# A hybrid convolution and state-space block on one core: what stands ahead of block 0, and where the rest of the modulation is made

## The chip, the cores and the metric

The kernel runs on one core of a Trainium2 chip. The metric is device time in microseconds (us), the median of several runs. Five engines work side by side, each through its own list in order: TensorE (PE, matmuls; its weight loads are PEld), VectorE (DVE), ScalarE (ACT), GpSimd (POOL) and SyncE (SP, which here only issues DMAs). Semaphores join the lists.

## The reference

One sequence of 2048 rows and width 1024 in float32, one layer. A vector `c` gives six modulation vectors of 1024 through `w_ada` (1024 x 6144, 24 MB):

```python
mod = (silu(c) @ w_ada + b_ada)
sh1, sc1, g1, sh2, sc2, g2 = split(mod, 6)
h = rmsnorm(x, norm1_g) * (1 + sc1) + sh1
u_conv, u_ssm, gl_conv, gl_ssm = split(h @ w_in)          # 1024, 512, 1024, 1024 columns
y_conv = silu(layernorm(causal_conv31(a * sigmoid(gate)))) @ conv_proj   # a, gate = split(u_conv)
y_ssm  = za * sigmoid(zb)      # za, zb = split(gelu(S5(u_ssm)) @ ssm_glu)
x = x + g1 * ((sigmoid(gl_conv) * y_conv + sigmoid(gl_ssm) * y_ssm) @ w_out)
h = rmsnorm(x, norm2_g) * (1 + sc2) + sh2
x = x + g2 * ((silu(f_gate) * f_up) @ w_ffn_out)          # f_gate, f_up = split(h @ w_ffn_in)
return rmsnorm(x, final_g)
```

S5 is a diagonal complex state space: 32 groups of 16 channels with 64 states each, computed in chunks of 8 steps. Its tables are made on the chip: an input matrix (`wm`), an output matrix (`vm`), the short kernel inside a chunk (`kst`), and the sine and cosine tables `sin_t`, `cos_t`.

## The kernel before

The sequence is worked in four blocks of 512 rows through the mixers (function `mixers`), then all rows go through the feed-forward part, which neither code nor diff touches here. Every float32 product of a layer is three matmuls (high by high, low by high, high by low: `three`, L1513 to L1515), so weights are split into `w_hi` and `w_lo`. A weight chunk is 512 KB. SP loads it into one of three `raw` buffers, POOL splits it with two instructions (L1793, L1795) into one of two slots, and PE uses it for 24 matmuls. POOL may split chunk w only when PE is done with chunk w-2. There are 48 chunks a block; here they are numbered 0 to 47.

On PE a block runs: four layers `us` (the S5 input), two pairs `ua`/`ug` (the gated convolution's input), `S` (state inputs, 4 quarters), two more pairs, gates `gl0` to `gl4`, a wait for the rotated states, `Y0` to `Y3` with a gate after each, gates to `gl15`, then `za`, `zb`, `cp`, and the output product with the transposes `h0` to `h7` of the next block's rows between. DVE runs: `u0`, 13 taps of the convolution, `u1`, 7 taps, then for each quarter q of the state the rotation `Rt`, `Rc`, `Rs` and the scan `sc` (L767 to L776), back-rotations `Dt`, `Dc`, `Ds` (L787 to L792), 104 more taps (L740), the low parts `ysl` of the S5 output (L558), and elementwise work. `u{m}` is one multiplication (L725) that waits for ACT's sigmoid of layer `ug{m}`. In the loop `u2` stands behind the scan of quarter 0 and `u3` behind that of quarter 2. PE's `Y0` waits for `Ds3`, its `za0` for `ysl3`.

Ahead of block 0 is the prologue. SP loads `w_ada` in 24 slabs of 1 MB into three buffers that lie over the `raw` and split buffers (`SLABS`, L1853); so weights of block 0 can be loaded only when the slabs are done. PE takes 20 slabs (`modulation`, L1445 and L1449), POOL four (L1769, L1763). Between them PE makes `h` of block 0 from transposed rows, transposes `wm`, and computes the `kst` tiles (L1505). DVE computes the tables in one long chain; each of its links waits for the one before. ACT stores `wm`, `vm` and `kst` to DRAM (L1107, L1109, L1113), from where SP loads them as needed. Every block's ACT list begins with a wait for these stores:

```python
act.wait_ge(wt_out, 16)
act.wait_ge(mat_out, 16 * (1 + T))
```

Blocks 0 to 2 are a hardware loop on PE, DVE and ACT (`Fori`), block 3 is written out; SP loops over all four.

Of the kernel before, what the change touches and what calls it, by code (L numbers as in the profile page):

```python
# [18 lines left out]
class Steps:  # L19

    def __init__(self, sem, phases):
        self.sem, self.at, self.base, self.per, self.names = sem, {}, {}, {}, {}
        total = 0
        for phase, times, segments in phases:
            n = 0
            names = []  # L30
            for seg, rep in segments:
                for j, name in enumerate(seg):
                    assert (phase, name) not in self.at, name
                    self.at[phase, name] = (n + j + 1, len(seg))
                names += seg
                n += len(seg) * rep
            self.base[phase], self.per[phase], self.names[phase] = total, n, names
            total += n * times
        self.next = {phase: 0 for phase, _, _ in phases}

    def step(self, phase, name):

        want = self.names[phase][self.next[phase]]
        assert want == name, f"{phase}: {name} where {want} stands"
        self.next[phase] += 1
        return self.sem, 1

    def again(self, phase):

        self.finished()  # L50
        self.next[phase] = 0

    def after(self, phase, b, name, it=0):

        at, width = self.at[phase, name]
        return self.sem, self.base[phase] + at + b * self.per[phase] + it * width

    def before(self, phase, b, name, it=0):

        at, width = self.at[phase, name]  # L60
        round_ = self.per[phase] if it is None else width
        v = self.base[phase] + at - round_
        assert v >= 0, (phase, name, v)
        return self.sem, v + b * self.per[phase] + (0 if it is None else it * width)

    def start(self, phase, b):

        return self.sem, self.base[phase] + b * self.per[phase]

    def finished(self):  # L70
        for phase, n in self.next.items():
            assert n in (0, len(self.names[phase])), (phase, self.names[phase][n])


def build(nc, x, c, w_ada, b_ada, norm1_g, w_in, conv_w, conv_b, conv_ln_g, conv_ln_b, conv_proj,
# [22 lines left out]
    ADA = 3  # L98


    SLABS = [("pe", k, h, r) for k in range(5) for h in range(2) for r in range(2)]
    for n, at in enumerate((2, 7, 12, 17)):
        SLABS.insert(at, ("pool", 5, n // 2, n % 2))
    last_slab = lambda kind: SLABS.index(("pe", kind, 1, 1))
    first_gate = last_slab(1) + 1
# [49 lines left out]
    with ExitStack() as ctx:  # L155
# [11 lines left out]
        def align():  # L167
# [20 lines left out]
            ("zero1", "eps1", "half_pi", "sign", "nsign")))  # L188
        ss, sd, rs, ss2, sd2, rs2 = (place(n, [P, TT], at=unit_at + 160 + 32 * i) for i, n in enumerate(
# [3 lines left out]
        bmod, c_in, ng = vt[:, 0:6 * KD], vt[:, 6 * KD:7 * KD], vt[:, 7 * KD:9 * KD]  # L193
# [88 lines left out]
        modrow = place("modrow", [4, HALF], at=ptmp_at)
        jexp = place("jexp", [P, T + 1, G])
        jer = place("jer", [P, T + 1, G])
        jei = place("jei", [P, T + 1, G])
        sv = place("sv", [P, 12, G])
        iota_i = place("iota_i", [P, NC + 1], I32)
        iota_f = place("iota_f", [P, NC + 1])
        cact = place("cact", [P, KD])
        dvec = place("dvec", [HG, G])  # L290
        cbc = place("cbc", [P, KD, P])
        ones = place("ones", [P, P])
        zc = place("zc", [P, KD, 7])
        ddiag = place("ddiag", [HG, G, HG])
        nat_v = place("nat_v", [6 * KD + 3 * KD + 3 * KC, P])
        nat_a = place("nat_a", [2 * G, P])
        nat_w = place("nat_w", [KC * TAPS, P])

        kst_at = end_kept - (T - 1) * G * HG * 4
        assert cursor[0] <= kst_at, (cursor[0], kst_at)  # L300
        kst = place("kst", [HG, G, 2 * T - 1, HG], at=kst_at)
        ada = [place(f"ada{s}", [P, KD // 2, HALF], at=raw_at + s * KD * HALF * 2) for s in range(ADA)]

        acc = place("acc", [P, 2, HALF], at=raw_at + ADA * KD * HALF * 2)
        bg = place("bg", [P, 2, D], at=dt_at)
        cursor[0] = h_at
        karg = place("karg", [P, 2, NC + 1, G])
        ktmp = place("ktmp", [P, NC + 1, G])
        jarg = place("jarg", [P, 2, T + 1, G])
        jtmp = place("jtmp", [P, T + 1, G])  # L310
        assert cursor[0] <= tr_at
# [17 lines left out]
        GY, GE = 5, 11  # L329
# [3 lines left out]
        pe_mix = [f"us{m}" for m in R(KS)] + [f"u{a}{m}" for m in R(2) for a in "ag"]  # L333
        pe_mix += [f"S{q}" for q in R(NQ)] + [f"u{a}{m}" for m in R(2, KC) for a in "ag"] + gl(0, GY)
        for q in R(NQ):
            pe_mix += [f"Y{q}", f"gl{GY + q}"]
        pe_mix += gl(GY + NQ, 2 * KD)
        for p in R(KD // 2):
            pe_mix += [f"za{m}" for m in pair(p)] + [["ln1"], ["ln2"], [], []][p] + [f"zb{m}" for m in pair(p)]
        pe_mix += [f"cp{m}" for m in R(KD)]  # L340
        for f in R(2):
            for j in R(KD // 2):
                pe_mix += [f"oc{f}{j}"] if j < KD // 2 - 1 else [f"o{f}{i}" for i in R(TT)]
                pe_mix += [f"h{k}" for k in TURN[j]] if f == 0 else []
# [10 lines left out]
        for q in R(NQ):  # L355
            act_mix += [f"Y{q}", f"gl{GY + q}"]
# [13 lines left out]
        for q in R(NQ):  # L370
            dve_mix += [f"Rt{q}", f"Rc{q}", f"Rs{q}", f"sc{q}"] + [["u2"], [], ["u3"], []][q]
# [1638 lines left out]
```

## Time and profile before

| | us |
|---|---|
| median of 3 runs | 2778.56 (2777.52 to 2779.61) |
| profiled execution, own time | 2779.5 |
| its span, first to last instruction | 2777.4 |
| PE busy | 2628.7 (95%) |
| DVE, ACT, POOL busy | 1508.4, 724.5, 1706.9 |
| mean granted PE clock | 0.973 of full speed |

Busy time is the union of an engine's instructions; issuing DMAs and waiting do not count. A timeline row gives start, duration, the line in the kernel's source, operation, output and inputs, and in brackets how long the engine was idle before it and what ended that. PE's instructions show two records for a plain float32 matmul.

### The profile page before, as it was taken

The page shows a single profiled execution, that of the slowest core. Times are in us where ns is not written, and L with a number is a line of the kernel's source. Part 1 is how long each engine was busy: PE and PEld are TensorE (multiplying, and loading weights), DVE is VectorE, ACT ScalarE, POOL GpSimd, SP SyncE. Part 2 cuts the span into 40 slices and gives each one's busy share as a digit, 9 for nine tenths or more (in the row PEclk, how much of TensorE's full clock was granted, in tenths as well). Part 3 has the DMA queues.
Part 4 walks back from the last instruction along what each step waited for, and adds up shares of the span by engine and source line. Part 5 has one row for each costly group of instructions (what it writes and reads, how often), then busy time and mean ns, then how long its engine had stood idle before and what let it go on. Part 6 is the DMA issues. An engine that isn't in the chain of part 4 may idle for free.

```text
span 2777.4 us, 32161 instructions
## 1 busy us (share of the span) xinstructions
PE 2628.7 (95%) x11735; PEld 2134.4 (77%) x11735; DVE 1508.4 (54%) x1772; ACT 724.5 (26%) x1116; POOL 1706.9 (61%) x1085
## 2 busy tenths in 40 slices
PE   4769999999999999999989999999999999999998
PEld 0347778878887878877868888878888878888886
DVE  6806975399629963597753334373333334735531
ACT  2210152103411232114533335443333321201100
POOL 2335465555666465546577776778777756766664
PEclk9888999999999999999999999999999999999999
DMA  8477443755276534835232232323222237556542
GB/s 259 167 197 149 113 148 121 176 152 159 92 194 148 158 106 138 195 111 187 82 115 87 73 107 85 120 69 91 73 88 87 73 110 258 185 178 192 169 128 76
DMA packets 422357, 376.20 MB, mean 135 GB/s; under 512 B 91752, under 2 KB 329528, under 8 KB 422072
## 3 DMA queue, kind: packets, MB, share of 16 engines
q1 hardware_dynamic: 312640, 294.69, 35.2%
q10 hardware_dynamic: 109560, 79.41, 10.8%
q8 instruction: 100, 1.64, 0.3%
q14 instruction: 57, 0.47, 0.1%
HBM read 311.06 MB, written 54.53 MB: 132 GB/s over the span
## 4 chain that ended last, share of the span: by engine, by line
PE 80%; DVE 10%; DMA 2%; ACTq 2%; issue 2%; POOL 2%; ACT 1%; DVEq 0%; SPq 0%; POOLq 0%
PE bank L1513 17%; PE bank L1515 17%; PE bank L1514 17%; PE bank L1718 5%; PE bank L1720 5%; PE bank L1719 5%; DVE wst L789 2%; PE bank L1634 2%; PE bank L1636 2%; PE bank L1635 2%; DVE bank L767 1%; PE bank L1575 1%; PE bank L1576 1%; PE bank L1562 1%; ACTq L1113 1%
## 5 line engine op out<-in xcount | busy, mean ns | idle before, releaser
L1793 POOL CAST w_hi<-raw 128x1024 fp32r<-128x1024 f32 x192 | 216.1, 1125 | 559.9 <-PE bank L1515 459.1
L1795 POOL TENSOR_TENSOR w_lo<-raw,w_hi 128x1024 fp32r<-128x1024 f32 x192 | 486.0, 2531 | 15.4
L1513 PE MATMUL bank<-h_hi,w_hi 128*128 128x512 f32 x896 | 356.9, 398 | 20.4 <-ACT uz L1142 19.4
L1514 PE MATMUL bank<-h_lo,w_hi 128*128 128x512 f32 x896 | 353.3, 394 | 0.0
L1515 PE MATMUL bank<-h_hi,w_lo 128*128 128x512 f32 x896 | 353.2, 394 | 0.0
L740 DVE SCALAR_TENSOR_TENSOR bank<-uc,cwt,bank 128x512 f32<-128x512 f32 x464 | 328.4, 752 | 8.0
L1812 POOL TENSOR_TENSOR fw_lo<-fsum,fw_hi 128x512 fp32r<-128x512 f32 x176 | 234.0, 1331 | 106.1 <-ACT fw_hi L1305 106.1
L1513 PE MATMUL bank<-xc_hi_T,fw_hi 128*128 128x512 f32 x704 | 276.2, 392 | 7.4 <-DVE tr L911 6.0
L1718 PE MATMUL bank<-ow_hi,hid_hi 128*128 128x512 f32 x704 | 274.6, 390 | 3.8 <-DVE hid_lo L971 3.8
L1515 PE MATMUL bank<-xc_hi_T,fw_lo 128*128 128x512 f32 x704 | 275.0, 391 | 0.0
L1514 PE MATMUL bank<-xc_lo_T,fw_hi 128*128 128x512 f32 x704 | 275.0, 391 | 0.0
L1719 PE MATMUL bank<-ow_hi,hid_lo 128*128 128x512 f32 x704 | 274.6, 390 | 0.0
L1720 PE MATMUL bank<-ow_lo,hid_hi 128*128 128x512 f32 x704 | 274.6, 390 | 0.0
L1513 PEld LDWEIGHTS bank<-h_hi,w_hi 128*128 128x128 f32 x896 | 171.8, 192 | 58.2 <-ACT uz L1142 19.8
L1513 PE MATMUL bank<-xc_hi_B,fw_hi 128*128 128x512 f32 x528 | 208.0, 394 | 7.2 <-issue 3.8
L1515 PE MATMUL bank<-xc_hi_B,fw_lo 128*128 128x512 f32 x528 | 207.0, 392 | 0.0
L1514 PE MATMUL bank<-xc_lo_B,fw_hi 128*128 128x512 f32 x528 | 206.9, 392 | 0.0
L1515 PEld LDWEIGHTS bank<-h_hi,w_lo 128*128 128x128 f32 x896 | 171.0, 191 | 36.7
L1514 PEld LDWEIGHTS bank<-h_lo,w_hi 128*128 128x128 f32 x896 | 171.4, 191 | 35.1
L971 DVE TENSOR_TENSOR hid_lo<-hraw,hid_hi 128x512 fp32r<-128x512 f32 x88 | 142.5, 1657 | 88.3 <-ACT hid_hi L1393 88.3
L1812 POOL TENSOR_TENSOR fw_lo<-raw,fw_hi 128x512 fp32r<-128x512 f32 x110 | 150.2, 1366 | 59.9 <-ACT fw_hi L1305 59.9
L1840 POOL TENSOR_TENSOR ow_lo<-raw,ow_hi 128x1024 fp32r<-128x1024 f32 x66 | 169.2, 2563 | 5.3
(291 smaller groups left out, 4975.6 us busy)
## 6 DMA issues: line engine op xcount, KB each, us to landing
raw<-in_w_in SPq DMA_DIRECT2D x112, 512.0 KB, 4.7
raw<-in_w_ffn_in SPq DMA_DIRECT2D x66, 512.0 KB, 5.5
raw<-in_w_ffn_out SPq DMA_DIRECT2D x66, 512.0 KB, 4.4
ada<-in_w_ada SPq DMA_DIRECT2D x24, 1024.0 KB, 5.2
hid_scratch<-tr SPq DMA_DIRECT2D x88, 256.0 KB, 2.6
hraw<-hid_scratch SPq DMA_DIRECT2D x88, 256.0 KB, 3.9
ssm_m<-vk_scratch SPq DMA_DIRECT2D x32, 512.0 KB, 4.9
raw<-in_ssm_glu SPq DMA_DIRECT2D x32, 512.0 KB, 3.6
```

Source lines behind the costliest of these rows:

```text
L740: ins = v.scalar_tensor_tensor(out=dst, in0=src, scalar=w, in1=conv_bank(m)[:], op0=ALU.mult, op1=ALU.add)
L971: v.tensor_tensor(hid_lo[n % RING][:], hraw[n % 4][:], hid_hi[n % RING][:].bitcast(F32), ALU.subtract).then_inc(hid_lo_done, 1)
L1513: t.matmul(dst, wh, xh, start=first, stop=False)
L1514: t.matmul(dst, wh, xl, start=False, stop=False)
L1515: return t.matmul(dst, wl, xh, start=False, stop=last)
L1718: t.matmul(dst, hid_hi[hs][:, cols], ow_hi[slot][:, wcols], start=(k == 0), stop=False)
L1719: t.matmul(dst, hid_lo[hs][:, cols], ow_hi[slot][:, wcols], start=False, stop=False)
L1720: ins = t.matmul(dst, hid_hi[hs][:, cols], ow_lo[slot][:, wcols], start=False, stop=(k == KF - 1))
L1793: g.tensor_copy(hi[:], src[:]).then_inc(hi_done, 1)
L1795: g.tensor_tensor(lo[:], src[:], hi[:].bitcast(F32), ALU.subtract).then_inc(split_done, 1)
L1812: g.tensor_tensor(fw_lo[i][:], part[WEIGHTS[i]], fw_hi[i][:].bitcast(F32), ALU.subtract)\
L1840: g.tensor_tensor(lo[:], src[:], hi[:].bitcast(F32), ALU.subtract).then_inc(ow_lo_done, 1)
```

## The change

The prologue keeps what block 0's first layer needs. Only `sh1` and `sc1` (8 slabs, 8 MB) are made there, by PE, with four buffers that lie in memory used later, so `raw` is free from the start. The small loads are reordered: `c` and the vectors, then `x`, then the S5 poles (`nat_a`), `log_dt` and the b inputs; four more kinds of small loads go to SP behind the first three weight chunks. `norm_roots`, `norm_scale` and ACT's statistics go ahead of the S5 tables. The transposition of `wm`, the c inputs, `sin_t`/`cos_t`, `vm`, `kst` and the DRAM stores go into block 0, among its input layers. On DVE the table work keeps its operands `first`, `second` and `part` in PSUM banks. In the DRAM copy of `kst` zeros are stored once, and each of the 8 stores of `kst` (ACT) writes only its non-zero part.

The other four modulation vectors are made one a block (`MADE`): eight slices of `w_ada` of 512 KB and the bias, broadcast, pass the `raw` ring, one behind each third weight chunk up to number 26. POOL multiplies each with its part of `silu(c)` and adds it into `acc` (`part_of_ada`), and PE sums over partitions behind `cp1` (`ad0`, `ad1`); ACT copies the result.

All loops over blocks are written out. In block 0 all four input pairs stand ahead of `S`, and seven gates instead of five stand ahead of `Y0`. In blocks 1 to 3 `u2` and `u3` move behind the scans of quarters 1 and 3.

```diff
-    ADA = 3
+    ADA = 4
+    SLABS = [(k, h, r) for k in range(2) for h in range(2) for r in range(2)]
...
+        MIX_CHUNKS.append(key)
+        if w % 3 == 2 and w // 3 <= KD:
+            MIX_CHUNKS.append(("ada", w // 3))
...
-        GY, GE = 5, 11
+        GY, GE = [7, 5, 5, 5], [12, 11, 11, 11]
...
+        MADE = ["g1", "sh2", "sc2", "g2"]
...
+            gated(0, 0)
+            dve.wait_ge(*scal.after("pro", "m8"))
+            link(v.tensor_copy(mag_k[:, :, 1:], mag_t[:].unsqueeze(2).broadcast_to([P, G, NC])))
+            dve.wait_ge(*tensor.after(0, "ct1"))
+            link(v.tensor_scalar(bank[4][:], bank[4][:], nsign[:, 0:1], None, ALU.mult))
+            link(v.tensor_scalar(bank[5][:], bank[5][:], -1.0, None, ALU.mult))
+            for j in R(4):
+                output_matrix(j)
+            gated(0, 1)
+            for j in R(4, T + 1):
+                output_matrix(j)
+            gated(0, 2)
...
-                    if q in (0, 2):
-                        gated(2 + q // 2)
+                    if b and q % 2:
+                        gated(b, 2 + q // 2)
...
+            def store_kernel():
+                act.wait_ge(pro_v, mark["kst"])
+                act.wait_ge(zeros_in, 16)
+                for t in R(T):
+                    act.dma_start(vk_d[t * HG:(t + 1) * HG, :, 1, t * HG:],
+                                  kst[:, :, 0:T - t, :].rearrange("p g s h -> p g (s h)")).then_inc(mat_out, 16)
...
-                act.wait_ge(wt_out, 16)
-                act.wait_ge(mat_out, 16 * (1 + T))
...
+                        if b == 0 and name == "us0":
+                            pe.wait_ge(*vec.after("pro", f"hl{k}"))
...
+                if b == 0:
+                    state_matrix()
+                    conv_input(*R(KC))
+                    kernel_tiles()
+                else:
+                    conv_input(0, 1)
...
+            def part_of_ada(b, n, k):
+                src = raw[n % RAW][:]
+                factor = cact[:, k:k + 1] if k < KD else part128[:, 0:1]
+                if k:
+                    g.tensor_scalar(src, src, factor, None, ALU.mult).then_inc(ada_scaled, 1)
+                    pool.wait_ge(ada_scaled, KD * b + k)
+                    pool.wait_ge(split_done, RAW + b * NMIX + ada_place[k - 1] + 1)
+                    g.tensor_tensor(acc[:], acc[:], src, ALU.add).then_inc(split_done, 1)
+                else:
+                    if b:
+                        pool.wait_ge(*tensor.after(b - 1, ad(b - 1)[-1]))
+                    g.tensor_scalar(acc[:], src, factor, None, ALU.mult).then_inc(split_done, 1)
```

PE from `sh1`/`sc1` to the first layer of block 0. Before, the slabs of the other vectors, the transposed `wm` and the `kst` tiles (`vm,b`) stand between `h` (the 32 transposes of `xs`) and the first layer:

```order
L1469 MATMUL bank<-ident,modrow 128x4 x4
L1476 MATMUL bank<-ident,cx 128x128 x8
L1459 MATMUL bank<-ident,xs 128x128 x32
L1445 MATMUL bank<-ada_245,cbc 128x512 x4
...
L1489 MATMUL bank<-ident,wm 128x128 x32
...
L1498 MATMUL bank<-acc,ones 128x512 x2
L1505 MATMUL bank<-vm,b_221 16x128 x32
...
L1513 MATMUL bank<-h_hi,w_hi_52 128x512
```

The change, same place; the rows of `wm` and `vm` stand behind 4 and 12 layers (`h_hi`, `w_hi`) of block 0:

```order
L1439 MATMUL bank<-ident,modrow 128x4 x4
L1452 MATMUL bank<-ident,xs 128x128 x32
L1423 MATMUL bank<-ident,nat_w 128x124
L1488 MATMUL bank<-h_hi,w_hi_52 128x512
...
L1467 MATMUL bank<-ident,wm 128x128 x32
L1473 MATMUL bank<-ident,cx 128x128 x8
L1488 MATMUL bank<-h_hi,w_hi_52 128x512
...
L1482 MATMUL bank<-vm,b_235 16x128 x32
L1543 MATMUL bank<-u_116,ssm_m_95 128x64 x8
```

So nothing but one transpose of the taps now stands between `h` and the first layer, and the `kst` tiles run directly ahead of `S`.

DVE in block 1, from the rotation of quarter 0; `dt_62` to `dt_65` are the quarters, `uc<-bank,tr_60` is `u2`. Before (a looped block):

```order
L767 TENSOR_TENSOR bank<-dt_62,sin_t 128x512
L769 TENSOR_TENSOR wst<-wst,cos_t 128x8x64
...
L725 TENSOR_TENSOR uc<-bank,tr_60 128x512
L767 TENSOR_TENSOR bank<-dt_63,sin_t 128x512
```

The change:

```order
L745 TENSOR_TENSOR bank<-dt_62,sin_t 128x512
L747 TENSOR_TENSOR wst<-wst,cos_t 128x8x64
L750 TENSOR_TENSOR wst<-wst,bank 128x8x64
L754 SCALAR_TENSOR_TENSOR wst<-mag_k,zero_70,wst 128x520
L745 TENSOR_TENSOR bank<-dt_63,sin_t 128x512
...
L644 TENSOR_TENSOR uc<-bank,tr_60 128x512
L745 TENSOR_TENSOR bank<-dt_64,sin_t 128x512
```

`u2` moved from ahead of quarter 1 to ahead of quarter 2.

POOL in block 0 of the change, where before there are only pairs of CAST and TENSOR_TENSOR of weight chunks:

```order
L1782 CAST w_hi_53<-raw_49 128x1024
L1784 TENSOR_TENSOR w_lo_55<-raw_49,w_hi_53 128x1024
L1761 TENSOR_SCALAR raw_50<-raw_50,vt 128x1024
L1764 TENSOR_TENSOR acc<-acc,raw_50 128x1024
L1782 CAST w_hi_52<-raw_51 128x1024
```

Behind each third split two instructions for `w_ada` stand in the list.

## Rows read from the trace of the kernel before

**Rows 1.** The page: busy time, share of the span and instructions of each engine.

```profile
PE 2628.7 (95%) x11735; PEld 2134.4 (77%) x11735; DVE 1508.4 (54%) x1772; ACT 724.5 (26%) x1116; POOL 1706.9 (61%) x1085
```

**Rows 2.** Windows: us; busy PE, PEld, DVE, ACT, POOL; clock; DMA share; GB/s. Blocks 0 and 1.

```profile
156.00:494.00 338.00, 306.51 (x1379) 255.44 (x1380) 202.26 (x251) 73.03 (x103) 174.17 (x96) 0.92 0.55 147
494.00:796.00 302.00, 294.14 (x1381) 245.31 (x1381) 208.47 (x256) 73.24 (x102) 173.13 (x96) 0.98 0.52 147
```

**Rows 3.** Timeline of PE in the prologue and block 0: start, us, operation, count, idle before.

```profile
15.39 0.34 PE L1433 MATMUL bank<-ident,nat_a 64*128 64x64 f32 x1 [15.39 <-DMA nat_w<-in_conv_w]
...
36.72 13.90 PE L1449 MATMUL bank<-ada,zc 128*4 128x512 f32 x32 [1.90 <-DMA ada<-in_w_ada]
...
100.71 7.19 PE L1445 MATMUL bank<-ada,cbc 128*128 128x512 f32 x16 [1.79 <-DMA ada<-in_w_ada]
...
123.58 3.71 PE L1489 MATMUL bank<-ident,wm 128*128 128x128 f32 x32
...
147.70 7.75 PE L1505 MATMUL bank<-vm,b 128*16 128x128 f32 x64
...
156.40 0.49 PE L1513 MATMUL bank<-h_hi,w_hi 128*128 128x512 f32 x1 [0.96 <-ACT kst L1102]
...
197.87 0.80 PE L1513 MATMUL bank<-h_hi,w_hi 128*128 128x512 f32 x1 [19.40 <-ACT uz L1142]
```

**Rows 4.** Timeline of ACT and its DMA issues (ACTq), end of the prologue.

```profile
157.19 30.92 ACTq L1113 DMA_DIRECT2D vk_scratch<-kst  x8
195.49 1.28 ACT L1142 ACT_TABLE_LOAD   x1 [39.42 <-DMA vk_scratch<-kst]
```

**Rows 5.** Timeline of PE: last layers of block 0, its end, and block 1.

```profile
378.14 0.49 PE L1513 MATMUL bank<-ys_hi,w_hi 128*128 128x512 f32 x1 [0.57 <-POOL w_lo L1795]
...
494.36 0.49 PE L1513 MATMUL bank<-h_hi,w_hi 128*128 128x512 f32 x1
...
538.00 1.22 PE L1562 MATMUL bank<-u,ssm_m 128*128 128x64 f32 x10
...
600.70 0.68 PE L1575 MATMUL bank<-wst,ssm_m 128*128 128x64 f32 x2 [6.09 <-DVE carry L797]
...
680.17 0.49 PE L1513 MATMUL bank<-ys_hi,w_hi 128*128 128x512 f32 x1 [0.64 <-ACT sg_s L1168]
```

**Rows 6.** Timeline of DVE in block 1: rotations, scans and what follows.

```profile
546.86 1.11 DVE L767 TENSOR_TENSOR bank<-dt,sin_t 128x512 f32<-128x512 f32 x1
...
556.90 0.69 DVE L725 TENSOR_TENSOR uc<-bank,tr 128x512 f32<-128x512 f32 x1 [5.85 <-ACT tr L1153]
557.51 3.36 DVE L767 TENSOR_TENSOR bank<-dt,sin_t 128x512 f32<-128x512 f32 x1
...
599.79 0.69 DVE L792 TENSOR_TENSOR wst<-wst,bank 128x512 f32<-128x512 f32 x1
...
675.26 4.69 DVE L558 TENSOR_TENSOR ys_lo<-tr,ys_hi 128x512 fp32r<-128x512 f32 x4
```

**Rows 7.** Windows, columns as before: the slab loads; GB/s is last.

```profile
25.00:50.00 25.00, 21.94 (x47) 4.13 (x48) 23.97 (x31) 3.38 (x6) 6.75 (x5) 1.00 0.90 317
```

**Rows 8.** Timeline of DVE in the prologue: the low parts of h.

```profile
82.26 0.69 DVE L558 TENSOR_TENSOR h_lo<-bank,h_hi 128x512 fp32r<-128x512 f32 x1
...
85.04 0.69 DVE L558 TENSOR_TENSOR h_lo<-bank,h_hi 128x512 fp32r<-128x512 f32 x1
```

**Rows 9.** Timeline of POOL in the same stretch: both halves of a weight chunk's split.

```profile
550.93 1.04 POOL L1793 CAST w_hi<-raw 128x1024 fp32r<-128x1024 f32 x1 [9.16 <-PE bank L1515]
552.05 2.39 POOL L1795 TENSOR_TENSOR w_lo<-raw,w_hi 128x1024 fp32r<-128x1024 f32 x1
556.37 1.04 POOL L1793 CAST w_hi<-raw 128x1024 fp32r<-128x1024 f32 x1 [1.93 <-PE bank L1515]
...
562.93 3.22 POOL L1795 TENSOR_TENSOR w_lo<-raw,w_hi 128x1024 fp32r<-128x1024 f32 x1
```

**Rows 10.** Windows, columns as before: PE behind its wait for the rotations; clock ahead of DMA share.

```profile
600.00:610.00 10.00, 9.30 (x38) 8.84 (x39) 9.61 (x16) 0.60 (x1) 0.00 (x0) 0.51 0.12 25
```

More of the change, by code:

```diff
@@ L66, in start, with step @@
-    def start(self, phase, b):
-        return self.sem, self.base[phase] + b * self.per[phase]
+        for stage, names in stages:
+            self.next[stage] = 0
+            for name in names:
+                total += 1
+                assert (stage, name) not in self.at, name
+                self.at[stage, name] = total
+    def step(self, stage, name):
+        want = self.names[stage][self.next[stage]]
+        assert want == name, f"{stage}: {name} where {want} stands"
+        self.next[stage] += 1
+        return self.sem, 1
@@ L294, in build @@
[L294 to L311, printed above, removed]
+        def early(at, end, *buffers):
+            cursor[0] = at
+            made = [place(*b) for b in buffers]
+            assert cursor[0] <= end, (buffers[0][0], cursor[0], end)
+            return made
@@ L894, in mixers @@
                     residual(1)
+                if MADE[b] == "sc2":
+                    dve.wait_ge(*scal.after(b, "ad0"))
+                    scale_of(1)
                 return residual
[L897 removed]
+            for b in R(NB - 1):
                 mixers(b)
[L899 removed]
             last_residual = mixers(NB - 1, last=True)
@@ L1453, in transposes @@
-            def transposes(phase, b, k, free=True):
+                t.transpose(dst[:, 0:rows], src[:], ident[0:rows, 0:rows]).then_inc(*tensor.step("pro", f"v{n}"))
+            pe.wait_ge(vectors_in, 7 * 16)
+            turn_rows_in(1, nat_v, bank[1])
+            pe.wait_ge(poles_in, 64)
+            turn_rows_in(0, nat_a, bank[0])
+            pe.wait_ge(pro_v, mark["zc"])
+            for n, (kind, half, rows) in enumerate(SLABS):
+                pe.wait_ge(ada_in[n % ADA], 16 * (n // ADA + 1))
+                for j in R(KD // 2):
+                    k, r = rows * KD // 2 + j, 2 * kind + half
+                    ins = t.matmul(bank[7][0:4, :], zc[:, k, 3 - r:7 - r], ada[n % ADA][:, j, :],
+                                   start=(r == 0 and k == 0), stop=(r == 3 and k == KD - 1))
+                ins.then_inc(*tensor.step("pro", f"ada{n}"))
@@ L1454, in transposes, with wait_bank @@
+            pe.wait_ge(pro_v, mark["modrow"])
+            for j in R(4):
+                ins = t.transpose(bank[7][:, 4 * j:4 * j + 4], modrow[:, j * P:(j + 1) * P], ident[0:4, 0:4])
+            ins.then_inc(*tensor.step("pro", "mt"))
+            def wait_bank(stage, name):
+                free = bank_free(stage, name)
                 if free:
-                    pe.wait_ge(*bank_free(phase, b, f"h{k}"))
+                    pe.wait_ge(*free)
+            def transposes(stage, k):
+                wait_bank(stage, f"h{k}")
```

1174 lines of the change are left out of this document (563 added, 611 removed).

## The prediction

> **What bounds the kernel now.** I read four views. The page first: PE is busy for 95% of the span [rows 1], so only two things can move the time much: where PE stands idle, and where it works at half clock. The windows by stage then show where that is: block 0 takes 338 us and PE is busy in 306.5 of them, block 1 takes 302 with 294.1 [rows 2]; and block 0 begins only at 156.40 [rows 3]. Blocks 2 and 3 take within 1 us of block 1. The timeline of PE tells what it does ahead of block 0: 16 matmuls (two records each), which are four slabs, in 13.90, the transposes of `wm` 3.71, the `kst` tiles 7.75, and long waits between; the wait of 19.40 at 178 is inside block 0 [rows 3]. The last is due to ACT: it issues the stores of `kst` for 30.92 us, stands idle 39.42 until they have landed, and reaches block 0's first own work at 195.49 [rows 4]. Last, the rows around one block [rows 5, 6]: PE waits 6.09 for the rotated states at 600.70, and DVE, busy otherwise through the rotations, waits 5.85 for ACT's `tr`, that is for `ug2`, which it had reached too early. `ysl3` ends at 675.26 + 4.69 = 679.95 and `za0` starts at 680.17: from the rotations on, DVE's chain and PE end almost together. So from the state inputs to `za0` DVE sets the pace, elsewhere PE.
>
> **Part 1, the slabs that stay.** Eight slabs in one stretch, all early. One slab costs 13.90/4 = 3.47 [rows 3]. Their loads fit: 317 GB/s came in while slabs were loaded [rows 7], 3.3 us for 1.05 MB, just under PE's 3.47. The first slab's matmuls stand behind the transpose of the poles `nat_a`. Before, small loads were in by 15.39 [rows 3]. Now 2 MB of `x` and four slabs, with the small ones 6.2 MB, are issued ahead or beside them: at 317 GB/s 19.6 us, plus some 2 until the first issue. Bounds 14 (they slip past) and 22 (they wait for all); I take 18.5, nearer to the end since most of it is issued earlier. With the transposes, slab 0 starts at 19.6. Eight slabs are 27.8, and the first cold ones 1.7 more (half clock, as in the stretch at 600 to 610 below): 49.1. Row to columns, `mod`, scale: 2.2, so 51.3.
>
> **Part 2, `h` and the first layer.** The transposes of `x` are paced by ACT and DVE together, 85.04 - 82.26 = 2.78 a tile [rows 8]. Eight tiles are 22.2, unless POOL contends: 73.5. The layer's matmuls run as tiles come, since PE now waits for each `hl`, so the first layer ends about 1.0 after the last tile, at 74.5. Before, the first layer ended at 156.40 + 5.44 = 161.8. This is 87.3 early, and the sum below has to say how much of it lives.
>
> **Part 3, block 0 up to the rotations.** A chunk takes 5.44, the distance of two CASTs that each wait for PE's bank, 556.37 - 550.93 [rows 9]. Three more `us` layers: 16.3, plus 2.7 of half clock after the thin stretch of transposes: 93.5. `wm` transposed: 3.71, the same for 8 c inputs about 2, with their waits on the copies 2 more: 101.2. Then eight chunks of `ua`/`ug`: 43.5, and about 1 where POOL has just done a part of `w_ada`: 145.7. The `kst` tiles 7.75 and switching 0.3, `S` 7.25 [rows 5]: 161. DVE's tables (`mag`, output matrices, `kst`) have 93.5 to 154 for work that before stood between other waits; I count them done at about 162 at the latest, so the rotations start at 162.5. The eight smaller stores leave ACT before `S` and no block list waits for all of them: the wait of 39.42 [rows 4] goes; the first load of `vm` back from DRAM is due only at `Y0`.
>
> From 546.86 to the end of `Ds3` (599.79 + 0.69) are 53.6 [rows 6]. In it are the 5.85 idle and two multiplications by 0.69 which in block 0 stand earlier: 53.6 - 5.85 - 1.4 = 46.4, `Ds3` ends at 208.9. PE has seven gates (38.1) for this time and ends them at 199 plus about 8 of waiting for a bank that ACT frees late; this is hidden. From 600.48 to `za0` are 679.95 - 600.48 = 79.5 in block 1; with 4 us less contention with POOL (4.69 for four low parts that cost 0.69 each, 2.8, alone, and others) about 78: `za0` at 286.9. PE waits there some 13 us, since its own layers between are no longer than before. From `za0` to the next block is 494.36 - 378.14 = 116.2 [rows 5]. The change adds two matmuls there, `ad0` and `ad1`; by the nearest row, 16 records or eight matmuls of the same 512 columns in 7.19 [rows 3], they take 1.8. Half clock behind the 13 us of idle: 2.7. So block 0 ends at 286.9 + 116.2 + 1.8 + 2.7 = 407.6, against 494.36: **86.8 gained**. So nearly all of the 87.3 lives: what block 0 saves on ACT's wait it gives back for the moved tables.
>
> **Part 4, blocks 1 to 3.** Moving `u2` behind quarter 1 takes the 5.85 out, if the chain behind is DVE's own. But POOL now has three more pairs (TENSOR_SCALAR, TENSOR_TENSOR) there. What the rows show of DVE beside POOL: `Rt` takes 1.11 alone and 3.36 when it starts beside a POOL instruction, and the low part of a weight takes POOL 2.39 alone and 3.22 beside DVE [rows 6, 9]. These operations exclude each other; the product at 599.79, which reads a bank, has 0.69 in the same busy stretch.
>
> The Trainium skill says the same in SBUF — State Buffer, section "SBUF: two separate sides": VectorE and GpSimd share a port pair there, and the lock holds for a whole instruction. By this rule the new POOL work would cost DVE its whole length where the two meet, 3.4 for each of three parts and so 7.2 a block more than I count below, 2712 in all; by the row one meeting costs 3.36 - 1.11 = 2.25, and not every part meets such an operation.
>
> A part of `w_ada` on POOL: the addition like `w_lo`, 2.39 (bound 3.22); the multiplication has no row. Bounds 1.04 (the CAST, which also reads one operand) and 2.39; I take 1.04, one operand being what it has in common with the CAST. So 3.4 a part. POOL needs 1.04 + 2.39 = 3.4 for a chunk and PE 5.44, so 2.0 are spare a chunk, 6.1 in three chunks, against 3.4 for a part: it fits on the average. But the split of chunk w can only start when PE is done with w - 2, so in the chunk behind a part POOL is late: 3.4 + 3.4 = 6.9 against 5.44 + 0. Such a part costs PE up to 6.9 - 5.44 = 1.4, and more beside DVE. In the rotations three parts fall; with DVE and POOL excluding each other DVE loses about 1 for each, 3 in all. So a block gains 5.85 - 3 = 2.9, the two `ad` matmuls cost 1.8: 1.2, in three blocks **3.6 gained**. Bounds for a block: +4 (nothing lost on POOL: 5.85 - 1.8) and -6.4 (each of three parts costs 3.5, that is 10.5, less 5.85, plus 1.8).
>
> The half clock behind PE's wait: at 600 to 610 it was granted 0.51, the 1.2 GHz level, after 6.09 of idle [rows 10]. If the wait shrinks to 3, this costs the same or less; I count nothing.
>
> SP loads nine slices a block more, 4.7 MB against the 147 GB/s × 302 us = 44 MB of a block [rows 2]; one takes 1.7 us at 317 GB/s and a chunk is due each 5.44 us, so the raw buffers stay ahead: 0.
>
> In block 3 of the kernel before, already written out, nothing runs slower than in the loop but for gaps of 1 us. Three more blocks written out: 2 us lost, bounds 0 and 3.
>
> **Sum.** 2777.4 - 86.8 - 3.6 + 2.0 = 2689.0 of span. The execution's own time is 2.1 above its span: 2691.1. The median lies 0.9 under the profiled execution: **2690**. The feed-forward part isn't touched, 1344 us as before. This forecast's own range: the poles ±4, the tables of DVE ending up to 10 later, the blocks +8 or -6 more: 2675 to 2708.
>
> **Rivals.** (B) POOL becomes the bound where parts are made. Each of the three parts in the rotations costs 3.5 in blocks 1 to 3, 31.5, of which 9 are counted: 22.5 more; in block 0, where DVE sets the pace, the same meetings cost 5: 2718. For it: `w_lo` beside DVE takes 3.22, CASTs likewise stretch. Against: POOL waits 1.93 for PE ahead of the CAST at 556.37, so there is slack [rows 9]. (C) Input comes early and the wait for the rotated states falls away: poles at 14 (-4.5), and in each of three blocks also the half clock behind the wait (5) and the loss to POOL not there: some -16 in all, 2674. For it: small loads were in at 15.39. (E) The store of `wm`, 2 MB in ACT's queue, takes ACT's time as the first `kst` store did; the issues took 30.92 for eight [rows 4], 3.9 each. Then `u0` and with it the rotations come up to 10 later: 2700.
>
> (D) The slower side: POOL starves PE throughout. The place is behind each third chunk, 36 in all: the part holds up the next split, PE waits, and wins nothing back, as POOL may not run ahead by more than two chunks. It decides from (86.8 + 3.6 - 2.0) / 36 = 2.5 us a part. If the multiplication costs what the addition does and both and the splits meet DVE each time, three chunks and a part need 3 × (1.04 + 3.22) + 2 × 3.22 = 19.2 of POOL against 16.3 of PE, 2.9 a part; with half clock behind some of the waits 3.5, 126 in all: about 2779 + 126 - 88 = 2817. Against it: DVE is busy in 208 of 302 us only [rows 2], largely on banks, and alone POOL has 2.0 spare a chunk.
>
> The Trainium skill, GPSIMD Engine Reference, section 4.1 on engine selection, says that one-operand work on this engine runs at about line rate and two-operand work about twice slower than on VectorE. By this the multiplication would be near the CAST's price, and (D) would be out. No row here shows a TENSOR_SCALAR on POOL.
>
> (F) The change doesn't do what it says: the first layer waits for something else, as the weight chunks on SP behind the 8 MB of slabs. Three chunks and 8 MB are 9.9 MB or 31 us at 317 GB/s, well ahead of 51; the first layer would have to wait until past 100. Then 2750.
>
> **Chances.** The forecast 0.62; B 0.13; C 0.12; E 0.09; D 0.02; F 0.02. The range of 8 in 10 takes in the forecast, E, most of C and most of B: 2668 to 2718. About 0.2%, or 5.6 us, is what a measurement of this kernel can tell from no change. D is slower; of the rest only a form of F could be within 0.2%. Faster 0.97, same 0.01, slower 0.02.
>
> **What would show it.** In the profile after: the first layer's last matmul at 74.5; `S` at 154; `Ds3` at 209 and `Y0` behind it; an idle of about 13 ahead of `za0` in block 0; the next block at 408. In blocks 1 to 3 302 minus 1; POOL's TENSOR_SCALAR at 1.04 (if 2.39, B gains); PE's idle rows released by POOL `w_lo` in the third chunks (B if above 1 each). ACT's first `uz` wait gone. Wrong is the forecast above all if DVE's tables aren't ready at 162 (then the rotations start late by as much, and everything behind), or if PE's wait ahead of `za0` is gone in favour of PE waiting at POOL.

## The result, and the profile after

The changed kernel takes 2760.32 us in the median of 5 runs (2753.51 to 2765.05) against 2778.56 of the kernel before (5 runs beside it); the ratio is 0.9927, 95% interval 0.9905 to 0.9949. It is faster by 0.7%, where 3.2% were forecast, and 2760.32 lies above the forecast range of 2668 to 2718. Repeated later, the same kernel gave 0.9911 (0.9879 to 0.9943) and 0.9915 (0.9881 to 0.9949). Medians and ratios are of fast runs: one execution of the version with narrow loads (3725.47) and one of the kernel before (10447.62) had granted clocks of 0.65 and 0.246 and are left out.

The profiled execution has a span of 2758.5 us. From the page, busy time of each engine (before in [rows 1]):

```profile
PE 2609.3 (95%) x11671; PEld 2136.7 (77%) x11671; DVE 1472.9 (53%) x1766; ACT 722.2 (26%) x1118; POOL 1852.2 (67%) x1134
```

POOL is busy 145 us more than before, PE 19 less. By window, columns as in [rows 2]; the windows are blocks 0 to 3:

```profile
64.00:410.00 346.00, 317.87 (x1489) 259.98 (x1490) 251.80 (x308) 85.49 (x121) 225.27 (x111) 0.96 0.55 152
410.00:734.00 324.00, 305.39 (x1398) 254.03 (x1397) 202.29 (x256) 70.83 (x101) 218.51 (x113) 0.95 0.52 151
734.00:1059.00 325.00, 306.36 (x1399) 254.51 (x1398) 202.22 (x257) 70.83 (x101) 218.07 (x114) 0.95 0.53 151
1059.00:1389.00 330.00, 308.60 (x1413) 255.58 (x1412) 216.79 (x263) 89.19 (x126) 223.64 (x116) 0.95 0.53 154
```

Block 0 begins at 64, not 156, and ends 2.2 us behind the forecast. The timeline of PE answers to [rows 3] and [rows 5]; start, us, operation, count, idle time before:

```profile
18.16 0.36 PE L1423 MATMUL bank<-ident,nat_a 64*128 64x64 f32 x1 [9.64 <-DMA nat_a<-in_ssm_a_im]
19.11 28.91 PE L1434 MATMUL bank<-ada,zc 128*4 128x512 f32 x64 [0.59 <-DVE zc L571]
...
64.07 0.77 PE L1488 MATMUL bank<-h_hi,w_hi 128*128 128x512 f32 x1 [1.50 <-issue]
...
289.58 0.80 PE L1488 MATMUL bank<-ys_hi,w_hi 128*128 128x512 f32 x1 [6.46 <-DVE ys_lo L534]
...
409.84 0.39 PE L1488 MATMUL bank<-h_hi,w_hi 128*128 128x512 f32 x1
```

The poles are in at 18.16 (forecast 18.5), the slabs end at 48.02 (49.1), `za0` starts at 289.58 (286.9) and block 1 at 409.84 (407.6), against 494.36: 84.5 us gained, 86.8 forecast. The wait of ACT for the stores [rows 4] is gone; its first work in block 0:

```profile
73.38 1.12 ACT L1108 ACTIVATE uz<-bank 128x512 f32<-128x512 f32 x1 [9.55 <-PE bank L1490]
74.53 0.36 ACTq L1112 DMA_DIRECT2D us_scratch<-uz  x1
```

Nearly everything that is missing is behind block 0. Block 1 lasts 324.1 us instead of 301.9, block 2 324.6 instead of 303.2, block 3 331.0 instead of 311.5 up to the first matmul of the feed-forward part, and that part 1369.0 instead of 1366.4. Block 1, cut at the same events in both traces:

| from, to | before | after | |
|---|---|---|---|
| first layer to `S` | 43.6 | 48.3 | +4.7 |
| `S` itself | 7.1 | 13.3 | +6.2 |
| `S` to `Y0` | 55.6 | 66.7 | +11.0 |
| `Y0` to `za0` | 79.5 | 78.1 | -1.3 |
| `za0` to the next block | 116.1 | 117.8 | +1.7 |
| sum | 301.9 | 324.1 | +22.2 |

PE's waits in block 1 of the changed kernel: what it waited for, us in total, times, the longest.

```profile
PE bank L1488 <- POOL w_lo L1784: 14.8, 5, 6.3
PE bank L1543 <- DMA u<-us_scratch: 2.8, 1, 2.8
```

The wait for the rotated states (6.1 in each block before, 5.9 in the last) is gone, as the change wants it. In its place stand two kinds that block 1 of the kernel before did not have: 14.8 us for POOL's `w_lo`, and 2.8 for the loads of `u` ahead of `S`. Where they stand, from PE's timeline and from POOL's in the rotations (before in [rows 9]):

```profile
458.14 0.32 PE L1543 MATMUL bank<-u,ssm_m 128*128 128x64 f32 x1 [2.79 <-DMA u<-us_scratch]
...
501.71 0.80 PE L1488 MATMUL bank<-h_hi,w_hi 128*128 128x512 f32 x1 [6.28 <-POOL w_lo L1784]
...
524.22 0.80 PE L1488 MATMUL bank<-h_hi,w_hi 128*128 128x512 f32 x1 [3.71 <-POOL w_lo L1784]
...
538.06 0.33 PE L1557 MATMUL bank<-wst,ssm_m 128*128 128x64 f32 x2
```

```profile
484.69 1.04 POOL L1782 CAST w_hi<-raw 128x1024 fp32r<-128x1024 f32 x1 [1.12 <-PE bank L1490]
485.81 2.39 POOL L1784 TENSOR_TENSOR w_lo<-raw,w_hi 128x1024 fp32r<-128x1024 f32 x1
488.17 4.67 POOL L1761 TENSOR_SCALAR raw<-raw,vt 128x1024 f32<-128x1024 f32 x1
492.93 3.61 POOL L1764 TENSOR_TENSOR acc<-acc,raw 128x1024 f32<-128x1024 f32 x1
496.49 1.98 POOL L1782 CAST w_hi<-raw 128x1024 fp32r<-128x1024 f32 x1
498.55 3.10 POOL L1784 TENSOR_TENSOR w_lo<-raw,w_hi 128x1024 fp32r<-128x1024 f32 x1
501.61 1.88 POOL L1782 CAST w_hi<-raw 128x1024 fp32r<-128x1024 f32 x1
503.56 3.09 POOL L1784 TENSOR_TENSOR w_lo<-raw,w_hi 128x1024 fp32r<-128x1024 f32 x1
```

The multiplication of a part takes 4.67 us here, beside DVE. Over 28 of the 32 parts that are added on, duration in ns (least, median, greatest):

```profile
L1761 POOL TENSOR_SCALAR raw<-raw,vt x28: 2838/2849/4674, 100.9 to 1226.9; 128x1024 f32<-128x1024 f32 x28
```

The median is 2.85, where the forecast took the CAST's 1.04 and bounded it by 2.39. A part is so 2.85 + 2.40 = 5.25 of POOL without contention, and three chunks and a part are 3 × 3.44 + 5.25 = 15.6 of PE's 16.3 us: only 0.7 is left for DVE's interference. From 484.69 POOL does not rest until 506.65. And at the three longest waits (2.8, 6.3 and 3.7) PE falls to half clock, for 17.1, 6.8 and 6.8 us; at those of 1.5 to 1.6 it does not. By window, from `S` on (clock ahead of the DMA share):

```profile
458.00:471.70 13.70, 13.56 (x65) 13.56 (x66) 8.68 (x13) 1.81 (x4) 4.17 (x3) 0.52 0.55 130
480.00:495.00 15.00, 15.00 (x68) 12.43 (x67) 11.05 (x9) 0.60 (x1) 13.64 (x6) 1.00 0.67 205
495.00:501.00 6.00, 0.43 (x2) 0.01 (x1) 5.96 (x6) 0.60 (x1) 5.92 (x3) 0.88 0.99 269
501.00:520.00 19.00, 18.29 (x71) 14.97 (x72) 18.69 (x18) 1.20 (x2) 15.64 (x7) 0.86 0.29 86
```

At half clock are 30.7 us of block 1 and 10.2 of block 1 before; half of the difference, 10 us, is by estimate what it costs. With PE's idle time, 18.6 against 7.9, and the two `ad` matmuls, 1.8, that makes 22.7, against the 22.2 found.

### The profile page after: what moved, and what is told of

Same layout as the page of the kernel before. It is cut to its first block, busy times and chain, and to the rows that moved or that the text cites. A ratio compares the mean times of both kernels' runs of the same rounds, so it can differ in the third digit from the quotient of the medians.

```text
span 2758.5 us, 30542 instructions
## 1 busy us (share of the span) xinstructions
PE 2609.3 (95%) x11671; PEld 2136.7 (77%) x11671; DVE 1472.9 (53%) x1766; ACT 722.2 (26%) x1118; POOL 1852.2 (67%) x1134
## 4 chain that ended last, share of the span: by engine, by line
PE 76%; DVE 8%; POOL 8%; DMA 4%; issue 1%; ACT 1%; ACTq 1%; DVEq 0%; POOLq 0%
PE bank L1488 16%; PE bank L1490 16%; PE bank L1489 16%; PE bank L1716 5%; PE bank L1717 5%; PE bank L1718 5%; POOL w_lo L1784 3%; DVE bank L711 2%; PE bank L1633 2%; PE bank L1635 2%; PE bank L1634 2%; POOL raw L1761 2%; PE bank L1543 2%; POOL w_hi L1782 1%; POOL acc L1764 1%
## 5 line engine op out<-in xcount | busy, mean ns | idle before, releaser
L1488 PE MATMUL bank<-h_hi,w_hi 128*128 128x512 f32 x896 | 367.3, 410 | 64.9 <-POOL w_lo L1784 60.4
L1489 PE MATMUL bank<-h_lo,w_hi 128*128 128x512 f32 x896 | 360.3, 402 | 0.0
L1490 PE MATMUL bank<-h_hi,w_lo 128*128 128x512 f32 x896 | 359.2, 401 | 0.0
L1490 PEld LDWEIGHTS bank<-h_hi,w_lo 128*128 128x128 f32 x896 | 175.3, 196 | 38.7
```

The lines of the kernel that those rows point to most:

```text
L1488: t.matmul(dst, wh, xh, start=first, stop=False)
L1489: t.matmul(dst, wh, xl, start=False, stop=False)
L1490: return t.matmul(dst, wl, xh, start=False, stop=last)
```

## The experiments

Two theories were held. **P**: a part on POOL costs 5.25 and not 3.4 us, and most where DVE rotates; PE waits for `w_lo`. **D**: a slice ahead of them in the ring of raw buffers pushes the four loads of `wm` (2 MB) to a later time, where they meet the store and the loads of `u`, and `S` is late. The kernel before ran beside each group of them; ratios are to it.

| kernel | median | before | ratio (95%) |
|---|---|---|---|
| changed, two more times | 2752.75, 2753.64 | 2774.08, 2780.07 | 0.9911, 0.9915 |
| parts of 32 columns | 2715.40 | 2774.08 | 0.9791 (0.9758 to 0.9824) |
| multiplication as copy | 2735.20 | 2778.93 | 0.9830 (0.9786 to 0.9874) |
| slices' loads of 32 columns | 2743.12 | 2774.08 | 0.9877 (0.9839 to 0.9915) |
| `wm` a chunk earlier | 2735.77 | 2774.08 | 0.9843 (0.9795 to 0.9891) |
| before, `wm` a chunk later | 2812.07 | 2778.93 | 1.0104 (1.0072 to 1.0137) |
| parts later | 2735.72 | 2780.07 | 0.9839 (0.9815 to 0.9864) |
| both | 2712.30 | 2778.93 | 0.9749 (0.9696 to 0.9802) |
| `u2`, `u3` back | 2767.94 | 2778.93 | 0.9937 (0.9914 to 0.9959) |
| both, `u2`, `u3` back | 2734.15 | 2780.07 | 0.9826 (0.9797 to 0.9855) |
| both, other places | 2714.23 | 2780.07 | 0.9749 (0.9714 to 0.9783) |

For the first of the two repeats this was on record:

> The changed kernel once more, so that the others of this call have it on the same chip. Both theories: 2755 to 2765.

and for the second:

> The changed kernel again, for this call's comparisons: 2750 to 2765.

It measured 2752.75, 2 under its range, and 2753.64, inside: medians of one kernel differ by some 7 us from group to group, so the ratios are what is compared.

### POOL's part, taken away

```diff
-                    g.tensor_scalar(src, src, factor, None, ALU.mult).then_inc(ada_scaled, 1)
+                    g.tensor_scalar(src[:, 0:32], src[:, 0:32], factor, None, ALU.mult).then_inc(ada_scaled, 1)
...
-                    g.tensor_tensor(acc[:], acc[:], src, ALU.add).then_inc(split_done, 1)
+                    g.tensor_tensor(acc[:, 0:32], acc[:, 0:32], src[:, 0:32], ALU.add).then_inc(split_done, 1)
```

> Of every w_ada part but the first, POOL multiplies and adds only 32 of 1024 columns (the rest of the four modulation vectors is left out); every load, wait and place stays. Theory P (POOL's part, 2.85 + 2.40 us instead of the 3.4 of the forecast, starves PE in blocks 1 to 3, and half clock follows each wait): PE's waits for w_lo, 14.8 us a block, fall under 3, with some 4 of half clock, so 16 a block, 2710 in all; the wait of 2.8 ahead of S with S at half clock stays. Theory D (the slices' DMA and the ring's order cost the time): 2750 to 2760.

2715.40, ratio 0.9791 against 0.9911: 33 us of 2774, where some 50 were expected. PE's waits in its blocks 1 and 2:

```profile
PE bank L1543 <- DMA u<-us_scratch: 3.7, 1, 3.7
PE bank L1488 <- POOL w_lo L1784: 1.7, 1, 1.7
...
PE bank L1488 <- DVE ys_lo L534: 6.1, 1, 6.1
PE bank L1543 <- DMA u<-us_scratch: 4.9, 1, 4.9
```

The 14.8 for `w_lo` are 1.7 in block 1, and the wait ahead of `S` stays, rather longer (3.7 and 4.9). Theory P holds, and D's wait is not a consequence of POOL. In block 2 a new wait of 6.1 for `ys_lo` appears ahead of `za0`: with PE no longer late, DVE's chain sets the pace there. So less came back than 16 a block: blocks 1 to 3 are shorter by 14.6, 9.3 and 9.7. Block 0 is shorter too, 335.6 us instead of 345.8 (346.7 and 340.1 in the changed kernel's repeats), so the parts were not free there.

### The price of the multiplication alone

```diff
-                    g.tensor_scalar(src, src, factor, None, ALU.mult).then_inc(ada_scaled, 1)
+                    g.tensor_copy(src.bitcast(w_hi[0][:].dtype), src).then_inc(ada_scaled, 1)
```

> The multiplication of each part, but for the first, is exchanged for an in-place copy into the type of the high parts, the form whose price of 1.04 us the forecast took (the factors are left out of the sum, so four modulation vectors are others). Theory P: had the multiplication cost what was forecast, a part takes 3.4 instead of 5.25 of POOL, PE's waits for w_lo in blocks 1 to 3 fall from 15 to 7 a block and with them half the clock loss: 10 a block, 2723. The rival, that the number of POOL's instructions and its lock with DVE count and not their length: within 8 of the change, 2745 to 2760.

```profile
L1761 POOL CAST raw<-raw x32: 1029/1042/2035, 103.2 to 1227.9; 128x1024 fp32r<-128x1024 f32 x32
```

```profile
PE bank L1488 <- POOL w_lo L1784: 6.7, 2, 3.7
PE bank L1543 <- DMA u<-us_scratch: 5.0, 1, 5.0
```

With the forecast's price, PE waits 6.7 for POOL instead of 14.8, as expected; the time is 2735.20, 0.9830 against 0.9911 and 0.9915, 23 us less than the change. Expected were 2723; the rival's 2745 to 2760 is out. Part of what is short of it stands in the second row: `S` now waits 5.0. So the mis-sized term alone would have made the forecast wrong by about 23 us, and it would still have been wrong by some 47 without it.

### What makes `S` late

Each row is the same event in block 1, us from the block's first layer, read from the issues of SP and ACT and their landings. "Store" is the last store of `uz`.

| kernel | `wm` loads issued | store issued, landed | `u` loads issued | last landed | `S` starts, waited |
|---|---|---|---|---|---|
| before | 15.6 to 17.1 | 23.2, 28.2 | 28.2 to 32.4 | 41.8 | 43.6, 0 |
| changed | 20.7 to 22.3 | 23.1, 30.4 | 30.4 to 38.3 | 48.3 | 48.3, 2.8 |
| slices of 32 columns | 20.7 to 22.3 | 23.1, 30.1 | 30.2 to 38.7 | 49.3 | 49.3, 3.8 |
| `wm` a chunk earlier | 16.1 to 17.6 | 23.1, 28.5 | 28.5 to 34.5 | 46.3 | 46.3, 0.8 |
| before, `wm` later | 21.0 to 22.5 | 23.2, 31.0 | 31.0 to 39.1 | 47.6 | 47.8, 4.0 |
| both, other places | 15.3 to 16.8 | 23.1, 27.9 | 27.9 to 36.4 | 47.2 | 47.2, 3.5 |

The rows of issues behind the first two lines, the loads of `wm` in SP's queue and of `u` in ACT's, before and then after:

```profile
509.96 1.84 SPq L1888 DMA_DIRECT2D ssm_m<-wt_scratch  x4
...
522.56 5.12 ACTq L1149 DMA_DIRECT2D u<-us_scratch  x8
```

```profile
430.55 1.93 SPq L1895 DMA_DIRECT2D ssm_m<-wt_scratch  x4
...
440.27 8.91 ACTq L1117 DMA_DIRECT2D u<-us_scratch  x8
```

The change leaves the loads of `wm` ahead of weight chunk 7, but slices of `w_ada` now stand in the ring of three buffers with it: the load just ahead of the four, that of chunk 6, waits for the split of chunk 4 instead of chunk 3, so SP gets there 5 us later. The edit that moves them back, for blocks 1 to 3:

```diff
-                ahead = {7: [0, 1, 2, 3], 14: [4, 5, 6, 7], 21: [8, 9], 22: [10, 11]}
+                ahead = {6: [0, 1, 2, 3], 14: [4, 5, 6, 7], 21: [8, 9], 22: [10, 11]}
```

> In blocks 1 to 3 the four loads of wm (2 MB) are issued one weight chunk earlier, ahead of chunk 6. Theory D for the stretch before S (the added slices push these loads by one place in SP's list onto the store and loads of u): S starts without its wait of 2.8 us and at full clock, 7.3 instead of 13.5, 9 a block, 2734 in all. Theory P alone: the gap is a matter of POOL's late splits, nothing changes, 2755 to 2763.

2735.77, 0.9843 against 0.9911, 19 us of the 26 expected. The wait is 0.8 in block 1, 1.2 in block 2, 0.6 in block 3; but `S` still takes 11.9 in block 2, and 7.4 in blocks 1 and 3. POOL's waits stay at 15.1 and 14.8 in blocks 1 and 2. The same edit in the kernel before, the other way round:

```diff
-                ahead = {7: [0, 1, 2, 3], 14: [4, 5, 6, 7], 21: [8, 9], 22: [10, 11]}
+                ahead = {8: [0, 1, 2, 3], 14: [4, 5, 6, 7], 21: [8, 9], 22: [10, 11]}
```

> The kernel before, with the four wm loads one chunk later (ahead of 8) in every block. Theory D: the loads of u then land some 5 us later, S waits 3 and falls to half clock (6 more); the rotations are behind S and PE waits for them, so all of it counts: 9 in each of blocks 1 to 3, 2800. If the wm loads' place doesn't matter: 2772 to 2779.

2812.07, 1.0104: 29 us slower, expected were 9 in each of three blocks. `S` in block 1 of the kernel before, and with this edit:

```profile
538.00 7.25 PE L1562 MATMUL bank<-u,ssm_m 128*128 128x64 f32 x64
...
539.39 12.91 PE L1562 MATMUL bank<-u,ssm_m 128*128 128x64 f32 x64 [4.04 <-DMA u<-us_scratch]
```

There is no `w_ada` in its blocks and no part on POOL; the place of four loads alone brings the wait of 4.04 and `S` at 12.9. Theory D is shown in both directions. Whether the slices' own bytes matter too was tried with narrow loads:

```diff
-                    d, kind = dst[:], 2 + b
-                    src = ada_d[:, key[1], kind * D:(kind + 1) * D] if key[1] < KD else \
-                        b_ada[0][kind * D:(kind + 1) * D].partition_broadcast(P)
+                    d, kind = dst[:, 0:32], 2 + b
+                    src = ada_d[:, key[1], kind * D:kind * D + 32] if key[1] < KD else \
+                        b_ada[0][kind * D:kind * D + 32].partition_broadcast(P)
```

> The loads of the w_ada slices bring only 32 of 1024 columns (the modulation comes out of other data), each at its old place in SP's list and with all of POOL's work. If the slices' own bytes delay u: S's wait of 2.8 goes, 2734 in all. If it is their place in the list that pushes the wm loads: the wait stays above 1.5 us, 2750 to 2760.

2743.12, 0.9877 with an interval that overlaps the change's. `S` waits 3.8 and 3.3 in blocks 1 and 2 and not at all in block 3. The time is 7 under the range of the reading it supports. It is mostly the place, since `wm` and `u` are issued and `S` starts as late as in the change in two of three blocks; what share the bytes have is left open.

### Parts away from the rotations, and both repairs

```diff
+    ADA_AT = [2, 5, 8, 18, 21, 24, 27, 30, 33]
...
-        if w % 3 == 2 and w // 3 <= KD:
-            MIX_CHUNKS.append(("ada", w // 3))
+        if w in ADA_AT:
+            MIX_CHUNKS.append(("ada", ADA_AT.index(w)))
```

> Only the second half of the last version: the w_ada parts behind chunks 2, 5, 8, 18, 21, 24, 27, 30, 33, the wm loads at their place of the change. If the two repairs add up (2760 to 2712 together, of which the wm loads gave 17 to 25): 2728 to 2736, S with its wait of 2.8 or more and at half clock. If the second only works once S is on time: over 2745.

Together with the earlier `wm` loads:

> The wm loads one chunk earlier in blocks 1 to 3, and the w_ada parts behind chunks 2, 5, 8, 18, 21, 24, 27, 30, 33 instead of 2 to 26, so that none meets the rotations. Theory P with the rotations as the costly place (waits of 5.3 and 3.3 to 4.8 there against 1.6 elsewhere): those two waits and their half clock go, some 12 a block, against 3 for two parts at 1.6 in their new place; 2736 - 27 = 2709. Rival (a part costs the same anywhere): 2730 to 2738.

The parts alone give 2735.72 (0.9839, 21 us), with `S` still waiting 4.8 in block 1; both 2712.30 (0.9749, 46 us), expected 2709. The two repairs add up, 19 + 21 against 46, within the intervals. PE's waits in block 1 of the version with both:

```profile
PE bank L1489 <- DVE ys_lo L535: 6.6, 1, 6.6
PE bank L1489 <- POOL w_lo L1785: 5.1, 4, 1.6
PE bank L1544 <- DMA u<-us_scratch: 1.6, 1, 1.6
```

In blocks 1 to 3 of this version a part costs PE 1.6 at most and often nothing; inside the rotations it cost 5.3 to 6.3 and 3.3 to 4.8. The version computes the same function and has the lowest median here, 2.5% below the kernel before. What is late next in it is DVE's `ys_lo`, 6.6 a block.

Another choice of places was `ADA_AT = [5, 8, 18, 20, 22, 25, 28, 31, 34]`, with both repairs:

> Both repairs, with parts behind chunks 5, 8, 18, 20, 22, 25, 28, 31, 34: only one slice ahead of the wm loads, and more parts in the stretch where PE waits for DVE anyway. By theory D the wait ahead of S (1.56) goes, by theory P the parts at 20 and 22 are hidden under the 6.6: 2703 to 2708. If denser parts starve PE: 2715 to 2725.

2714.23, 0.9749: no better. The last row of the table above shows where it is lost: `wm` is early, but `S` waits 3.5, as the loads of `u` take as long to issue as in the change. A slice is now loaded at 31.9, in the middle of them; that this is the reason fits, but was not tried apart. Both bounds of the expectation missed the time by a little, and its reason was wrong. The parts at 20 and 22 took the place of most of the wait ahead of `za0`, of which 1.05 is left. And block 0, with no part behind chunk 2, takes 336.2 us instead of the 345.5 of the version with both repairs: what blocks 1 to 3 lose, it wins back in part.

### `u2` and `u3` at their old place

```diff
-                    if b and q % 2:
+                    if b and q % 2 == 0:
```

> u2 and u3 in blocks 1 to 3 back behind quarters 0 and 2, all else as changed. Theory P: Ds3 ends at 516 and PE reaches Y0 only at 538, so the 6 us that the old place costs DVE are hidden: 2750 to 2762. Rival (the move of u2 and u3 gives its 6 a block): 2770 to 2778.

> Both repairs, and u2 and u3 of blocks 1 to 3 back behind quarters 0 and 2. With POOL out of the way DVE's chain sets the pace again (PE waits 6.6 for ys_lo ahead of za0), so DVE's idle in the old place counts, some 6 a block: 2728. If the move never matters: 2705 to 2715.

In the changed kernel it gives 2767.94, 0.9937 (0.9914 to 0.9959) against 0.9911 and 0.9915 (0.9881 to 0.9949): the ratios differ by 6 to 7 us, the intervals overlap, no loss is shown and one of up to 0.6% can't be excluded, and the expectation of 2762 at most was missed by 6. `Ds3` ends there at 528, PE is at `Y0` at 543 and waits for nothing. In the changed kernel itself DVE still waits at `u2`, as in [rows 6], 3.84 where the forecast counted 5.85 as gone:

```profile
485.22 0.69 DVE L644 TENSOR_TENSOR uc<-bank,tr 128x512 f32<-128x512 f32 x1 [3.84 <-ACT tr L1121]
485.83 3.35 DVE L745 TENSOR_TENSOR bank<-dt,sin_t 128x512 f32<-128x512 f32 x1
```

With both repairs the same edit costs 0.9826 - 0.9749 = 0.8%, 21 us (2734.15 where 2728 was expected), and the wait for the rotations is back:

```profile
PE bank L1558 <- DVE wst L771: 5.9, 1, 5.9
```

So the move is worth about its 5.9 a block where POOL leaves DVE in charge; the rest of the 21 goes with half clock, part of it in `S` (11.6 in block 3, behind a wait of 0.98). In the changed kernel little or nothing of it is seen.

## Why the prediction was wrong, point by point

**Part 1 and 2, the prologue: right.** Slab 0 at 19.11 (19.6), slabs done at 48.0 (49.1), and the first layer's result is taken by ACT at 73.4 (74.5).

**Part 3, block 0: right in the number, partly by luck**, 409.84 against 407.6. `S` started at 159.3 (154), late by PE's waits for POOL, and the first rotation at 168.1 (162.5). But from there to the end of `Ds3` DVE took 42.1 us and not 46.4, so that `Ds3` ended at 210.2 (208.9): two errors of about 5 cancel. PE waited ahead of `za0` 6.5 and not 13, since it had waited for POOL at 183 (5.6) already. In the rotations DVE set the pace, so PE's waits for POOL were covered there. But the parts were not free: with 32 columns `S` starts at 154.7, DVE takes 36.9 from the first rotation to `Ds3`, and the block is 10 shorter, where the forecast had about 1 for POOL. What was counted at nothing there, the moved DVE tables, cost nothing: DVE waits 2.39 for `S` behind them.

**Part 4, blocks 1 to 3: wrong**, by 66.7 us: they took 63.1 longer together, where 3.6 less was forecast. Three steps failed. First, the price of the multiplication: "I take 1.04, one operand being what it has in common with the CAST". It took 2.85 alone and up to 4.67, and even the upper bound of 2.39, taken from a two-operand row, was too low. The nearest row by the number of operands was not the nearest by cost. Nor did the loss fall where it was looked for: two parts, not three, met the rotations of block 1, and DVE went through these in 44.0 us where 50.8 were forecast, but PE, starved by POOL, came later still. The rule of the Trainium skill, GPSIMD Engine Reference, section 4.1, that one-operand work is about line rate, fits the CAST (1.04) but not this TENSOR_SCALAR (2.85 for the same 128x1024): the measurement decides. By the copy experiment this step is 23 of the 70 us that the median is off.

Second, half clock: it was priced behind the wait for the rotations, "I count nothing" for a shorter one, and not at all behind POOL's waits and ahead of `S`. The rows for it were there (10 at half clock behind 6.09 of idle, [rows 10]): each new wait of some 3 us and more had to be charged about its own length again.

Third, SP's queue: "the raw buffers stay ahead: 0". The bytes mattered little, but the position did. Chunk 7 and with it four other loads came 5 us later, and the forecast asked only whether a slice arrives in time, not what stands behind it in SP's list. Moving only these loads gave back 19 us, and took 29 from the kernel before.

The two `ad` matmuls cost 1.7 (1.8 forecast). The 2 us for the written-out loops were not tried apart; the feed-forward part, 2.5 longer here, took between 1364.7 and 1369.6 in the profiles of all versions, so it tells nothing.

Three slips in the working changed little. 5.85 - 3 - 1.8 is 1.05 a block and not 1.2. Block 3 did not take within 1 us of block 1, but 311.5 against 301.9. And the terms of C add up to more than its 16: 4.5 for the poles and three times 5 for the clock are 19.5 already.

**The rivals.** B had the mechanism, parts that starve PE in the rotations, and the right place, but 3.5 a part, where the two in the rotations cost 5.3 to 6.3 and 3.3 to 4.8 and as much again in clock. C was half right: the wait for the rotations did vanish, though the poles were in at 18.2 and not 14; PE was simply never early enough to meet it. D's rule (all 36 parts) didn't hold: in blocks 1 to 3 a part outside the rotations costs 0 to 1.6, sometimes up to 3.0. E, ACT's queue behind the store of `wm`, did not show: with parts of 32 columns the first rotation starts at 163.2, 0.7 behind the forecast. F is out, the first layer waits for nothing but `h`.

The Trainium skill, SBUF — State Buffer, section "SBUF: two separate sides", with its port pair held for a whole instruction, fits these runs: a CAST of 1.04 takes 1.9 and the multiplication 4.67 beside DVE's two-operand work, and the part shifted out of the rotations takes 2.85 and 2.40 again.

What stays open: the 22 us between the version with both repairs (2712) and the forecast (2690). Its profile has 5.1 of POOL waits and 6.6 of waiting for `ys_lo` a block; none of it was taken away by itself. Narrow parts and earlier `wm` loads were not run together; taken one by one they gave 33 and 19 of the 70.

## What to carry to other kernels

An operation that no row shows has no upper bound in a row of another kind; on an engine with 2 us to spare a chunk, the forecast must say what happens at three times the price. An item added to a shared ring or queue moves all that is tied to a position in it: compute the new issue time of each of these, and look at what is in flight then. And here a wait of 3 to 6 us in a dense stretch of PE cost about twice its length, so work for a side engine belongs where no third engine competes with it.

## What the hardware showed that was not expected

POOL's multiplication by a per-partition factor, 128x1024 float32, takes 2.85 us, more than its two-operand addition (2.40) and 2.7 times its CAST (1.04); beside DVE's rotations it took up to 4.67.

Half clock came behind shorter idle times than the kernel before had shown: ahead of `S` the wait was 1.18 in block 2 of the version with the earlier `wm` loads, and `S` took 11.9 instead of 7.3, while in blocks 1 and 3 of the same run, behind 0.78 and 0.60, it took 7.4. In the kernel before a wait of 1.01 ahead of `S` in block 3 left it at 7.3. In the version with both repairs one of 1.56 in block 1 left it at 7.4, and with `u2` and `u3` back one of 0.98 gave 11.6. So between 1.0 and 1.6 both outcomes were seen, and the length of one wait does not decide it alone.
